# Second down product of a transformer kernel: last quarter of its depth by seven block products, final norm and output in column pieces

## The chip, the cores and the metric

The kernel runs on one core of one Trainium2 chip. The metric is the device time in microseconds (us) of one execution; the text writes ns where a number is in nanoseconds. Engines are named as in the profile: PE is TensorE's matmuls, PEld its weight loads, DVE is VectorE, ACT ScalarE, POOL GpSimd, SP SyncE, whose queue here only issues DMAs.

## What is computed

Two transformer blocks on 1024 tokens of width 1024, in fp32. The part that the change touches is the end of the second block and a small piece in its middle:

```python
def sqrelu_mlp(h, ln_g, w1, w2):
    u = rmsnorm(h, ln_g) @ w1            # 1024 -> 4096
    return jnp.square(jax.nn.relu(u)) @ w2   # 4096 -> 1024
...
        h = h + sqrelu_mlp(h, ln_ff_g[l], w_ff1[l], w_ff2[l])
    return rmsnorm(h, ln_final_g)
```

with `rmsnorm(x, g) = x * rsqrt(mean(x*x) + 1e-6) * g` over the 1024 features of a token. The small piece is the same norm over 128 values for each of four heads inside `bidirectional_gla`.

## The kernel before, in words

**Layout.** Activations lie with the feature on the partitions: `XB` holds the residual stream as eight row tiles of 128 features, each 1024 tokens wide. Every fp32 product is made of three passes: each operand is split into a high part (a rounding copy on ACT) and a low part (a subtraction on DVE), and PE adds high*high, high*low and low*high. A 128x128 weight block against 512 tokens is thus three matmuls.

**Two ways to make a product.** A *plain unit* (`pe_unit`, `product`, line 256) makes one row tile of the output, all 1024 tokens, from eight weight blocks: 8 x 3 x 2 = 48 matmuls of 512 columns. The *seven* way (`Seven` for the up products, `Down` for the down products) treats two row tiles by two column halves as a 2x2 block matrix and makes the four quarters of the result with seven block products instead of eight (the table `FACTORS`: weight factors A11, S1, S2, S4, S3, A12, A22 against data factors B11, T1, T2, B22, T3, B21, T4). S1 to S4 are sums of weight quarters made on DVE (`dve_dws`, lines 2639 to 2652, for the down product). T1 to T4 are sums of data quarters.

**Down product.** Its depth of 4096 is cut into groups of 1024. For each group `g` there are seven factors `i` and for each factor four products `p` (row pairs of the output), so 28 products of 12 matmuls of 512 columns (`pe_down_seven`, line 3143, its matmuls at 3158). Before, three groups go this way (`DOWN2_GROUPS = FF2_GROUPS - 1`, 84 products), and the last quarter of the depth is made by eight plain units (`pe_ff2_down`, line 3171); the last two of these, at line 3187, run in the column pieces 0:512, 512:768 and 768:1024 (`END_COLS`).

**Hidden layer and its sums.** The up product (`Seven` S2, `pe_seven`, matmuls at 3136) makes the 32 hidden tiles as 16 pairs `q`, seven products each. ACT squares the two tiles of a pair (`act_up_square`, 2559), SP stores them to the HBM array `hidden` (2859). For pairs 0 to 11 DVE also makes T1 to T4 with four operations of 512 columns in its slots 1, 2 and 3 of the next pair (`dve_t_sums`, 2539), into the tiles `TSUM`, and SP stores them in two DMAs of 512 KB to `hidden_t` (2875).

**Order of the work.** Nothing schedules at run time. Each engine runs a list written out by hand: a *slot* is one product of PE, and for it ACT makes a high weight part three products ahead (`act_dpw_hi`), DVE the low part (`dve_dpw_lo`, 2636), then ACT and DVE split one quarter `k` of the next data block (`act_block_hi`, `dve_block_lo`, 2620), then DVE makes a weight sum (`dve_dws`) and adds a finished product to `XB` (`dve_quad`, 2661). The engines are held together by semaphores, and a wait stops everything behind it on its engine.

**From the up to the down product.** In the last pair of the up product (`q = 15`, "slot 15,i" for its product i) the first data block B11 of the down product is loaded by SP (`sp_block`, 2910) as soon as product 15,0 is done, then four weight tiles of 1 MB (`sp_w4`, 2894) after 15,1 and 15,2, then blocks 1 and 2. ACT splits block 0 from slot 3 on (`HI_FIRST`); DVE makes the low parts of the first weights and of block 0 at the end of its slots 4, 5 and 6 (`dve_dpw_lo`, `dve_block_lo`). At the head of the same DVE slots stand the sums of the up product: `dve_sum12` (2411) in slot 4, `dve_sum22` (2417) in slot 5, for which PE's product 15,6 waits, `dve_sum11` (2421, 2428) in slot 6, `dve_sum21` (2438, 2439) after it. ACT's square of the last tile and its next high weight part follow `dve_sum21`.

**The end.** Each finished row tile is squared (ACT), the squares are added (DVE), PE multiplies the sum by a constant matrix, which leaves the mean over all features on every partition (3198, 3199), ACT takes the root as Ln (2774) and Exp (2776, scale -0.5), and DVE multiplies `XB` by weight and root into `Y` (3110), one operation for each row tile and piece. SP stores each at once (3248). In the head norm of `act_gla` the root is Ln (2029) and Exp (2032) as well.

## Time and profile before

| | |
|---|---|
| median of 3 runs | 2974.15 us (2974.0 to 2974.2) |
| profiled execution: its own time, its span | 2975.5 us, 2973.7 us |
| PE busy | 2909.8 us, 98% of the span |
| PEld, DVE, ACT, POOL busy | 81%, 67%, 48%, 16% |
| chain that ended last, by engine | PE 89%, DVE 4%, ACT 4%, issue 2% |
| DMA | 262.14 MB, mean 88 GB/s |

The page of the profile gives busy times by engine; a PE that is busy 98% of the span is not thereby at its peak, since its matmuls overlap. The chain follows the work back from the last instruction. The timeline and the stretches give start times from the start of the span.

### The profile page before, as it was taken

Reading aid. Unit: us, or ns where it says so; the run is one execution under the profiler, and the core shown is the slowest. Engines: PE = TensorE matmul, PEld = TensorE weight load, DVE = VectorE, ACT = ScalarE, POOL = GpSimd, SP = SyncE. Lnnn points to the kernel's source line nnn. Section 1 sums busy time; section 2 is a strip of 40 time slices with the busy share of each in tenths; the row PEclk is TensorE's granted clock in tenths of the full one; section 3 lists DMA queues with packets and bytes.
Section 4 is the critical chain, followed back from the end, with each engine's and each line's share of the span. In section 5 each row is a group of like instructions: output and inputs, shape, how many; then the busy total and the mean of one; then the engine's idle time right before and its main releaser. Section 6 shows DMA issues by size and latency. Waiting matters only on the chain.

```text
span 2973.7 us, 42637 instructions
## 1 busy us (share of the span) xinstructions
PE 2909.8 (98%) x16332; PEld 2413.5 (81%) x16332; DVE 1984.1 (67%) x3262; ACT 1441.8 (48%) x2411; POOL 467.7 (16%) x764
## 2 busy tenths in 40 slices
PE   9999999889999999999999999999999999999998
PEld 6888888778988887888878888777877788888887
DVE  6653246766775349999989852475654877778864
ACT  4552125887776126555444431375643544444432
POOL 0110004765554120000000010261012000000000
PEclk9999997999999999999999999999999999999999
DMA  4222231000000511333344332000101244464232
GB/s 150 73 84 71 85 114 43 2 1 2 2 2 7 207 43 64 114 114 114 114 160 157 116 111 92 28 2 36 43 30 72 104 165 168 157 241 156 99 114 71
DMA packets 85383, 262.14 MB, mean 88 GB/s; under 512 B 10448, under 2 KB 13648, under 8 KB 84800
## 3 DMA queue, kind: packets, MB, share of 16 engines
q1 hardware_dynamic: 74208, 219.29, 20.3%
q0 software_dynamic: 10976, 40.15, 3.8%
q8 instruction: 131, 2.15, 0.3%
q14 instruction: 68, 0.56, 0.1%
HBM read 187.58 MB, written 66.06 MB: 85 GB/s over the span
## 4 chain that ended last, share of the span: by engine, by line
PE 89%; DVE 4%; ACT 4%; issue 2%; POOL 0%; DMA 0%; SPq 0%; ACTq 0%; DVEq 0%; POOLq 0%
PE PS L256 33%; PE PS L3136 23%; PE PS L3158 12%; PE PS L919 3%; PE PS L933 3%; PE PS L905 2%; PE PS L904 2%; PE PS L280 1%; PE PS L1563 1%; PE PS L1598 1%; PE PS L1585 1%; ACT P_SHORT L1003 1%; PE PS L956 1%; PE PS L3187 1%; ACT PT L1013 1%
## 5 line engine op out<-in xcount | busy, mean ns | idle before, releaser
L223 ACT CAST WHI<-RAW 128x1024 fp32r<-128x1024 f32 x100 | 104.8, 1049 | 589.4 <-PE PS L256 569.6
L228 DVE TENSOR_TENSOR WLO<-RAW,WHI 128x1024 fp32r<-128x1024 f32 x102 | 125.5, 1231 | 361.4 <-ACT WHI L223 360.1
L256 PE MATMUL PS<-HLO,WHI 128*128 128x512 f32 x992 | 306.2, 390 | 0.0
L3136 PE MATMUL PS<-XSH_T,PWH 128*128 128x512 f32 x596 | 233.1, 391 | 5.4 <-DVE PWL L2396 2.4
L3136 PE MATMUL PS<-XSH_T,PWL 128*128 128x512 f32 x596 | 231.9, 389 | 0.0
L3136 PE MATMUL PS<-XSL_T,PWH 128*128 128x512 f32 x596 | 231.9, 389 | 0.0
L3158 PE MATMUL PS<-DXH,PWH 128*128 128x512 f32 x560 | 218.1, 389 | 1.4 <-DVE DXL L2620 1.3
L256 PEld LDWEIGHTS PS<-HLO,WHI 128*128 128x128 f32 x992 | 186.5, 188 | 39.2
L3158 PE MATMUL PS<-DXL,PWH 128*128 128x512 f32 x560 | 217.9, 389 | 0.0
L3158 PE MATMUL PS<-DXH,PWL 128*128 128x512 f32 x560 | 217.9, 389 | 0.0
L3136 PE MATMUL PS<-XSH_B,PWL 128*128 128x512 f32 x456 | 177.4, 389 | 0.0
L3136 PE MATMUL PS<-XSH_B,PWH 128*128 128x512 f32 x456 | 177.4, 389 | 0.0
L3136 PE MATMUL PS<-XSL_B,PWH 128*128 128x512 f32 x456 | 177.4, 389 | 0.0
L256 PE MATMUL PS<-HHI,WHI 128*128 128x512 f32 x512 | 160.5, 395 | 2.7 <-DVE WLO L228 2.7
L256 PE MATMUL PS<-HHI,WLO 128*128 128x512 f32 x512 | 158.4, 391 | 0.0
L2392 ACT CAST PWH<-WS_S 128x512 fp32r<-128x512 f32 x148 | 91.4, 617 | 129.1 <-PE PS L3136 115.8
L904 PE MATMUL PS<-KHD,QS 128*128 128x512 f32 (+3 forms) x384 | 138.8, 368 | 3.7 <-DVE KF L388 2.2
L3136 PEld LDWEIGHTS PS<-XSH_T,PWH 128*128 128x128 f32 x596 | 111.9, 188 | 30.8 <-DVE PWL L2396 4.2
L1114 POOL TENSOR_SCALAR P_LONG<-P_LONG,HINV,GATE 128x640 f32<-128x640 f32 (+3 forms) x128 | 121.5, 960 | 93.6 <-DVE HINV L1097 92.8
L1003 ACT ACTIVATE P_LONG<-P_LONG,HMIN 128x640 f32<-128x640 f32 (+3 forms) x128 | 116.8, 914 | 38.1 <-DVE HMIN L1092 37.4
L3136 PEld LDWEIGHTS PS<-XSH_T,PWL 128*128 128x128 f32 x596 | 111.9, 188 | 23.5
L3136 PEld LDWEIGHTS PS<-XSL_T,PWH 128*128 128x128 f32 x596 | 111.9, 188 | 23.4 <-issue 0.5
(443 smaller groups left out, 7225.6 us busy)
## 6 DMA issues: line engine op xcount, KB each, us to landing
W<-in_w SPq DMA_DIRECT2D x57, 1024.0 KB, 6.4
RAW<-in_w SPq DMA_DIRECT2D x104, 512.0 KB, 3.3
hidden<-W SPq DMA_DIRECT2D x54, 512.0 KB, 2.8
DXR<-hidden_t SPq DMA_DIRECT2D x20, 1024.0 KB, 5.1
DXR<-hidden SPq DMA_DIRECT2D x15, 1024.0 KB, 5.1
hidden_t<-W SPq DMA_DIRECT2D x24, 512.0 KB, 3.3
...
```

What stands on the lines that cost most here:

```text
L223: nc.scalar.copy(WHI[:, slot, :], RAW[:, slot, :]).then_inc(w_hi, 1)
L228: nc.vector.tensor_tensor(WLO[:, slot, :], RAW[:, slot, :], WHI[:, slot, :].bitcast(F32), ALU.subtract).then_inc(w_lo, 1)
L256: last = nc.tensor.matmul(o[:, half], w[:, slot, cols], x(k)[:, half], start=(k == 0 and w is WHI and x is hi), stop=(done and k == kcs - ...
L904: nc.tensor.matmul(out, QS[s % 2][:, j, :], KHD[g][:, branch, c:end], start=True, stop=False)
L905: last = nc.tensor.matmul(out, QS[s % 2][:, j, :], KLD[g][:, branch, c:end], start=False, stop=True)
L919: last = nc.tensor.transpose(turn_ps(c)[:, P * (2 * x + e):P * (2 * x + e) + P], src, IDENT[:, :])
L933: last = nc.tensor.matmul(out_ps(m)[half_of(e), :], (VS, VW)[branch][:, kt, g], PT[u % 8][:, 2 * x + e, :], start=False, stop=(u + 1 == us ...
L1003: nc.scalar.activation(p, p, ACT.Exp, scale=-1.0, bias=HMIN[:, n % 8, branch:branch + 1], accum_out=HSUM[:, n % 8, branch:branch + 1]).the ...
L1114: nc.gpsimd.tensor_scalar(p, p, HINV[:, n % 8, branch:branch + 1], GATE[:, qt, col:col + 1], ALU.mult, ALU.mult).then_inc(p_done, 1)
L2392: nc.scalar.copy(c.pwh[n % 4][:, :], c.raw_of(n)).then_inc(pw_hi, 1)
L3136: last = nc.tensor.matmul(c.banks[q % 2][b], wt[n % 4][:, cols], xt[x][:, k, :], start=(opens and k == 0 and xt is c.xsh and wt is c.pwh), ...
L3158: last = nc.tensor.matmul(DOWN_BANK(i, p), wt[:, cols], xt[:, k, :], start=(opens and k == 0 and wt is d.pwh(n) and xt is d.xh[r]), stop=( ...
```

## The change

The last quarter of the down product becomes a fourth group of the seven way: `DOWN2_GROUPS = FF2_GROUPS`. The eight plain units, their eight weight splits and eight data splits go. T sums are made and stored for all 16 pairs, those of pairs 12 to 14 in the up product, those of pair 15 in slots 1 to 3 of the down product. In SP's list the sums of pair 14 stand ahead of the first block load. The seventh factor of the last group (A22, T4) runs in two column pieces of 256; its eight pieces of 12 matmuls are followed by reads of PE's result in the order of `dve_end`. The residual columns 512:1024, finished one factor earlier, are squared in the slots of factors 4 and 5. The squares are added by POOL. The pieces of norm and output are columns 512:1024, 0:256, 256:512. Roots, here and in the head norm, are Sqrt on ACT and a reciprocal on DVE. Of the output rows of the first piece the last two are made by ACT and POOL.

```diff
@@ -2026,10 +2026,8 @@
-            nc.scalar.activation(ORS[:, h, :], OSUM[:, h, :], ACT.Ln, scale=1.0 / GLA_DV, bias=EPS_T[:, 0:1])\
+            nc.scalar.activation(ORS[:, h, :], OSUM[:, h, :], ACT.Sqrt, scale=1.0 / GLA_DV, bias=EPS_T[:, 0:1])\
                 .then_inc(gl_root, 1)
-            act.wait_ge(gl_root, 2 * h + 1)
-            nc.scalar.activation(ORS[:, h, :], ORS[:, h, :], ACT.Exp, scale=-0.5).then_inc(gl_root, 1)
...
     def dve_gla_norm(dve, h):
-        dve.wait_ge(gl_root, 2 * h + 2)
+        dve.wait_ge(gl_root, h + 1)
+        seq(dve, nc.vector.reciprocal(ORS[:, h, :], ORS[:, h, :]))
...
-    DOWN1_GROUPS, DOWN2_GROUPS = FF1_GROUPS - 1, FF2_GROUPS - 1
+    DOWN1_GROUPS, DOWN2_GROUPS = FF1_GROUPS - 1, FF2_GROUPS
...
@@ act_ff2_down @@
             if g == DOWN2_GROUPS - 1:
...
+                for m in END_SQUARES_AT.get((i, p), ()):
+                    act_end_square(act, m)
+                if (i, p) == (5, 2):
+                    for k in range(KC - N_POOL_ROWS, KC):
+                        act_prescale(act, k)
+                if (i, p) == (6, 0):
+                    break
+        for n in (11, 12, 13):
+            act_end_square(act, n)
+        act_end_root(act, 0)
+        for n in (14, 15, 16, 17):
+            act_end_square(act, n)
+        act_end_root(act, 1)
+        for n in (18, 19):
+            act_end_square(act, n)
+        act_end_root(act, 2)
@@ sp_seven2, for q in range(Q_LAST2) @@
             for b in range(2):
                 store(q, b)
-            if q < T2_PAIRS:
-                sp.wait_ge(t_sums, T_SUMS0 + 4 * q + 4)
-                for b in range(2):
-                    sp.dma_start(hidden_t[q, b], TSUM[b][:, :]).then_inc(D2.t_out, 16)
+            sp.wait_ge(t_sums, T_SUMS0 + 4 * q + 4)
+            for b in range(2):
+                sp.dma_start(hidden_t[q, b], TSUM[b][:, :]).then_inc(D2.t_out, 16)
         sp.wait_ge(pw_lo, S2.done(Q_LAST2 - 1, 6))
         sp.wait_ge(sums_done, S2.sums)
         sp.wait_ge(prod_done, S2.done(Q_LAST2, 0))
@@ sp_block @@
-            sp.wait_ge(d.t_out, d.t_out0 + 32 * 4 * d.groups)
+            sp.wait_ge(d.t_out, d.t_out0 + 32 * pairs.stop)
@@ sp_ff2_down, after the weights of group 1 @@
+        sp.wait_ge(t_sums, T_SUMS0 + 4 * FF2_PAIRS)
+        for b in range(2):
+            sp.dma_start(hidden_t[Q_LAST2, b], TSUM[b][:, :]).then_inc(D2.t_out, 16)
...
+    HI_END, END_A, END_B = HI_COLS, slice(0, 256), slice(256, 512)
+    END_PIECES = (HI_END, END_A, END_B)
...
+    def act_end_root(act, i):
+        cols = END_PIECES[i]
+        n = cols.stop - cols.start
+        act.wait_ge(end_mean, END_MEAN0 + i + 1)
+        nc.scalar.activation(ROOT[:, cols], bank(END_BANK[i])[:, 0:n], ACT.Sqrt, bias=EPS_T[:, 0:1]).then_inc(end_root, 1)
+
+    def pool_end(pool):
+        for r, n in enumerate(END_SUMMED):
+            cols, k = END_SQUARES[n]
+            if r == END_SUMMED_IN[1]:
+                pool.wait_ge(end_rstd, END_RSTD0 + 1)
+                for j in range(N_POOL_ROWS):
+                    y = Y[:, KC - N_POOL_ROWS + j, HI_END]
+                    pool.wait_ge(prescaled, PRESCALED0 + j + 1)
+                    nc.gpsimd.tensor_tensor(y, y, END_RSTD_HI, ALU.mult).then_inc(scaled_by_pool, 1)
+            pool.wait_ge(end_sq, END_SQ0 + n + 1)
+            if r:
+                pool.wait_ge(end_sum, END_SUM0 + r)
+            nc.gpsimd.tensor_tensor(END_SUM[:, cols], END_SUM[:, cols], SQ_RING[r % 4][:, 0:cols.stop - cols.start],
+                                    ALU.add).then_inc(end_sum, 1)
+
+    def dve_end_z(dve, p):
+
+        row = XB[:, 2 * p + 1, END_B]
+        dve.wait_ge(prod_done, D2.prod0 + 28 * (DOWN2_GROUPS - 1) + 16 + p + 1)
+        nc.vector.tensor_tensor(row, row, bank(4 + p)[:, END_B], ALU.add).then_inc(end_z, 1)
+
+    def dve_end_quad(dve, b, p):
+
+        cols, at_bank = ((END_A, 4), (END_B, 0))[b]
+        row = XB[:, 2 * p + 1, cols]
+        dve.wait_ge(end_prod, END_PROD0 + 4 * b + p + 1)
+        if b:
+            dve.wait_ge(end_z, END_Z0 + p + 1)
+        nc.vector.tensor_tensor(row, row, bank(at_bank + p)[:, END_A], ALU.add).then_inc(end_quad, 1)
+
+    def dve_end_rstd(dve, i):
+        cols = END_PIECES[i]
+        dve.wait_ge(end_root, END_ROOT0 + i + 1)
+        nc.vector.reciprocal(RSTD_END[i], ROOT[:, cols]).then_inc(end_rstd, 1)
+        dve.wait_ge(end_rstd, END_RSTD0 + i + 1)
+        if i:
+            dve.wait_ge(end_quad, END_QUAD0 + 4 * i)
+        else:
+            dve.wait_ge(D2.quads, quad_at(4, 3))
+
+    def dve_end_scale(dve, i, rows):
+        for k in rows:
+            nc.vector.scalar_tensor_tensor(Y[:, k, END_PIECES[i]], XB[:, k, END_PIECES[i]], NORM_W[:, 4, k:k + 1],
+                                           RSTD_END[i], ALU.mult, ALU.mult).then_inc(y_done, 1)
+
+    def dve_end(dve):
+        for p in range(3):
+            dve_end_quad(dve, 0, p)
+        dve_end_rstd(dve, 0)
+        dve_end_scale(dve, 0, range(0, 2))
+        dve_end_quad(dve, 0, 3)
+        dve_end_scale(dve, 0, range(2, 4))
+        dve_end_quad(dve, 1, 0)
+        dve_end_scale(dve, 0, range(4, 5))
+        dve_end_quad(dve, 1, 1)
+        dve_end_scale(dve, 0, range(5, 6))
+        dve_end_quad(dve, 1, 2)
+        dve_end_rstd(dve, 1)
+        dve_end_scale(dve, 1, range(0, 2))
+        dve_end_quad(dve, 1, 3)
+        dve_end_scale(dve, 1, range(2, KC))
+        dve_end_rstd(dve, 2)
+        dve_end_scale(dve, 2, range(KC))
+
+    def pe_end_mean(pe, i):
+        cols = END_PIECES[i]
+        out = bank(END_BANK[i])[:, 0:cols.stop - cols.start]
+        pe.wait_ge(end_sum, END_SUM0 + END_SUMMED_IN[i])
+        pe.wait_ge(end_sq, END_SQ0 + (8, 16, 20)[i])
+        pe.wait_ge(end_quad, END_QUAD0 + i + 1)
+        last = nc.tensor.matmul(out, ONES[:, :], END_SUM[:, cols], start=True, stop=(i == 0))
+        if i:
+            last = nc.tensor.matmul(out, ONES[:, :], SQ_LAST[:, cols], start=False, stop=True)
+        last.then_inc(end_mean, 1)
+
+    def pe_end_product(pe, b, p):
...
+        cols, at_bank = ((END_A, 4), (END_B, 0))[b]
...
+            for wt, xt in ((D2.pwh(n), D2.xh[r]), (D2.pwh(n), D2.xl[r]), (D2.pwl(n), D2.xh[r])):
+                last = nc.tensor.matmul(bank(at_bank + p)[:, END_A], wt[:, w], xt[:, k, cols],
...
+    def pe_end(pe):
+        for b in range(2):
+            for p in range(4):
+                pe_end_product(pe, b, p)
+                if p == 1:
+                    pe_end_mean(pe, b)
+        pe_end_mean(pe, 2)
@@ dve_seven2 @@
             dve_seven_slot(dve, S2, j)
-            if 1 <= q <= T2_PAIRS:
+            if q:
                 dve_t_sums(dve, q - 1, i)
@@ dve_ff2_down, at the end of a slot @@
+            if g == 0 and i == 0 and p:
+                dve_t_sums(dve, Q_LAST2, p)
+            if (g, i) == (DOWN2_GROUPS - 1, 5):
+                dve_end_z(dve, p)
+            if (g, i, p) == (DOWN2_GROUPS - 1, 6, 0):
+                break
+        dve_end(dve)
...
```

## Rows read from the trace of the kernel before

**Rows 1.** Stretches by stage: us, busy us (count) by engine, PEclk, DMA share, GB/s
```profile
2627.30:2643.70 16.40, 16.40 (x74) 13.56 (x73) 8.98 (x13) 7.91 (x14) 0.00 (x0) 1.00 1.00 385
...
2656.40:2872.30 215.90, 215.89 (x952) 178.75 (x953) 186.27 (x284) 93.34 (x159) 0.00 (x0) 1.00 0.39 142
2872.30:2937.60 65.30, 65.30 (x290) 54.07 (x289) 22.67 (x20) 14.49 (x14) 0.00 (x0) 1.00 0.12 45
2937.60:2962.90 25.30, 25.17 (x152) 21.86 (x151) 12.36 (x18) 11.63 (x15) 0.00 (x0) 1.00 0.18 66
```

**Rows 2.** Chain that ended last, from 2840 us: start, us, what
```profile
2872.31 65.28 PE PS L256 x288
2937.59 12.31 PE PS L3187 x60
...
2950.01 1.10 PE PS L3198 x2
...
2951.96 5.75 PE PS L3187 x48
...
2962.92 0.43 DVE XB L3099
...
2963.81 1.28 ACT L2774
...
2965.59 1.28 ACT L2776
...
2967.34 0.48 DVE Y L3110
```

**Rows 3.** Timeline of SP, its DMA issues: start, us, line, out<-in, count
```profile
2578.51 0.93 SPq L2875 DMA_DIRECT2D hidden_t<-W  x2
...
2627.33 0.37 SPq L2910 DMA_DIRECT2D DXR<-hidden  x1
2629.84 3.60 SPq L2894 DMA_DIRECT2D W<-in_w  x4
```

**Rows 4.** Timeline of ACT around the third weight tile of the down product
```profile
2641.74 0.62 ACT L2632 CAST PWH<-W 128x512 fp32r<-128x512 f32 x1 [2.26 <-DMA W<-in_w]
```

**Rows 5.** Timeline of DVE in slots 15,5 and 15,6
```profile
2638.01 0.69 DVE L2417 TENSOR_TENSOR W<-PART,PS 128x512 f32<-128x512 f32 x1 [0.27 <-PE PS L3136]
...
2642.59 0.68 DVE L2636 TENSOR_TENSOR PWL<-W,PWH 128x512 fp32r<-128x512 f32 x1
```

**Rows 6.** Chain that ended last, from 2627 us: the first factor of the down product
```profile
2647.31 0.69 DVE PWL L2636
...
2648.61 0.61 DVE S L2644
...
2656.41 3.74 PE PS L3158 x15
```

**Rows 7.** Groups of DVE instructions by line: all reciprocals but those of 2 elements
```profile
L1688 DVE RECIPROCAL NINV<-NSUM 128x1 f32<-128x1 f32 x64 | 9.8, 154 | 0.4 <-ACT PN L1628 0.4
...
L1174 DVE RECIPROCAL CINV<-CSUM 128x8 f32<-128x8 f32 x15 | 3.0, 203 | 0.5
```

**Rows 8.** Timeline of DVE at the end, the output rows of two pieces
```profile
2956.98 5.38 DVE L3110 SCALAR_TENSOR_TENSOR Y<-XB,NORM_W,W 128x512 f32<-128x512 f32 x8
...
2963.59 3.25 DVE L3110 SCALAR_TENSOR_TENSOR Y<-XB,NORM_W,W 128x256 f32<-128x256 f32 x8
```

**Rows 9.** Groups of POOL instructions by line and form: one addition of 512 columns
```profile
L2292 POOL TENSOR_TENSOR XSR_T<-XB 128x512 f32<-128x512 f32 x4 | 5.5, 1379 | 0.1
```

**Rows 10.** Waits of DVE around the head norm: us in total, times, longest us
```profile
DVE ON L2056 <- ACT ORS L2032: 3.8, 2, 1.9
```

**Rows 11.** Stretches of 4 us around short stops of PE (columns as rows 1)
```profile
36.00:40.00 4.00, 1.32 (x6) 0.94 (x6) 3.27 (x4) 2.43 (x5) 0.00 (x0) 0.97 0.04 12
40.00:44.00 4.00, 4.00 (x13) 3.15 (x12) 3.93 (x7) 0.00 (x0) 0.00 (x0) 0.60 0.38 139
44.00:48.00 4.00, 4.00 (x16) 2.64 (x15) 2.54 (x4) 0.07 (x1) 0.00 (x0) 1.00 0.30 115
```

More of the change, by code:

```diff
@@ L2280, in build @@
               [x_in_used(3), x_in_used(4)], hid2_hi, hid2_lo, hid_hi, 28 * DOWN1_GROUPS + FF1_REST, x_in[2],
-              x_in_used(2), [R + 32 * KB + 8 * KB * k for k in range(4)] +
-              [X_AT + 16 * KB, X_AT + 24 * KB, R, R + 8 * KB], FF2_TILES - KC, KC)
+              x_in_used(2), [], 0, 0)
     TSUM = [W[0], W[2]]
@@ L2910, in sp_block, with sp_ff2_down @@
         sp.dma_start(d.xr[b % 4][:, :, :], src).then_inc(d.block_in[b % 4], 16)
-    def sp_plain2(sp, k):
-        sp.wait_ge(hid_out[k % 2], 16 * ((FF1_TILES, 0)[k % 2] + FF2_PAIRS))
-        if k >= 4:
-            sp.wait_ge(prod_done, D2.prods - (12, 12, 8, 8)[k - 4])
-            sp.wait_ge(D2.lo, 4 * D2.blocks + k - 3)
-        else:
-            sp.wait_ge(D2.lo, 4 * (D2.blocks - 4 + k) + 4)
-        sp.dma_start(D2.plain_raw[k][:, :], hidden[FF2_TILES - KC + k]).then_inc(D2.block_in[(D2.blocks + k) % 4], 16)
-    def sp_ff2_down(sp, load):
+    def sp_ff2_down(sp):
         sp.wait_ge(up_done, S2.ups)
@@ L2933, in sp_ff2_down @@
                 for p in range(4):
-                    sp_w4(sp, D2, 2, p)
-        for k in range(2):
-            sp_plain2(sp, k)
-        sp.wait_ge(pw_lo, D2.prods - 8)
-        for t in range(2):
-            u = U_FF2 + t
-            sp.dma_start(RAW[:, u % 2, :], a["w"][stored_down(FF2_TILES - KC + t)]).then_inc(w_loaded[u % 2], 16)
-        for k in range(2, KC):
-            sp_plain2(sp, k)
-        for t in range(2, KC):
-            load(U_FF2 + t, stored_down(FF2_TILES - KC + t))
@@ new lines, in build @@
+    END_SUMMED = [n for n, (cols, k) in enumerate(END_SQUARES) if n != 0 and n != KC and not (n >= 12 and k == 7)]
+    END_SUMMED_IN = (7, 13, 16)
+    SQ_RING = [W[0][:, LO_COLS], W[0][:, HI_COLS], W[3][:, LO_COLS], W[3][:, HI_COLS]]
+    SQ_LAST, END_SUM, ROOT = W[4][:, HI_COLS], W[2], W[1]
+    END_RSTD_HI = W[4][:, LO_COLS]
+    END_RSTD_LO = sb("END_RSTD_LO", [512], R + 96 * KB)
+    RSTD_END = [END_RSTD_HI, END_RSTD_LO[:, END_A], END_RSTD_LO[:, END_B]]
+    end_sq, end_sum, end_mean, end_root, end_rstd = sq_done, acc_done, mean_done, ln_done, rstd_done
@@ new lines, in act_end_square @@
+    def act_end_square(act, n):
+        cols, k = END_SQUARES[n]
+        act.wait_ge(*final_at(n))
+        if n in END_SUMMED:
+            r = END_SUMMED.index(n)
+            if r >= 4:
+                act.wait_ge(end_sum, END_SUM0 + r - 3)
+            dst = SQ_RING[r % 4][:, 0:cols.stop - cols.start]
+        elif n >= 12:
+            dst = SQ_LAST[:, cols]
+        else:
+            dst = END_SUM[:, cols]
+        nc.scalar.activation(dst, XB[:, k, cols], ACT.Square).then_inc(end_sq, 1)
@@ new lines, in pe_end_product @@
+    def pe_end_product(pe, b, p):
+        n, r = D2.n - 4 + p, (D2.blocks - 1) % 4
+        cols, at_bank = ((END_A, 4), (END_B, 0))[b]
+        pe.wait_ge(pw_lo, D2.prod0 + n + 1)
+        if b:
+            pe.wait_ge(D2.quads, quad_at(5, p))
+        else:
+            pe.wait_ge(end_z, END_Z0 + p + 1)
+            pe.wait_ge(D2.quads, quad_at(4, p))
+        for k in range(4):
+            if b == p == 0:
+                pe.wait_ge(D2.lo, 4 * (D2.blocks - 1) + k + 1)
+            w = slice(k * P, k * P + P)
+            for wt, xt in ((D2.pwh(n), D2.xh[r]), (D2.pwh(n), D2.xl[r]), (D2.pwl(n), D2.xh[r])):
+                last = nc.tensor.matmul(bank(at_bank + p)[:, END_A], wt[:, w], xt[:, k, cols],
+                                        start=(b == 1 and k == 0 and wt is D2.pwh(n) and xt is D2.xh[r]),
+                                        stop=(k == 3 and wt is D2.pwl(n)), skip_group_check=True)
+        last.then_inc(end_prod, 1)
@@ L3141, in pe_seven, with pe_down_seven @@
                 pe_mean(pe, c.norm)
-    def pe_down_seven(pe, d, z_free):
-        for n, (g, i, p) in enumerate(d.products):
+    def pe_down_seven(pe, d, z_free, end):
+        for n, (g, i, p) in enumerate(d.products[:end]):
             opens = i in (0, 1, 5)
@@ L3243, in _ @@
         sp_seven2(sp)
-        sp_ff2_down(sp, load)
-        for i, (a0, a1) in enumerate(END_COLS):
+        sp_ff2_down(sp)
+        for i, cols in enumerate(END_PIECES):
             for k in range(KC):
-                sp.wait_ge(y_done, KC * i + k + 1)
-                sp.dma_start(out[k][:, a0:a1], Y[:, k, a0:a1]).then_inc(out_done, 16)
-        sp.wait_ge(out_done, 16 * KC * len(END_COLS))
+                if i == 0 and k >= KC - N_POOL_ROWS:
+                    sp.wait_ge(scaled_by_pool, POOL_SCALED0 + k - (KC - N_POOL_ROWS) + 1)
+                else:
+                    sp.wait_ge(y_done, KC * i - (N_POOL_ROWS if i else 0) + k + 1)
+                sp.dma_start(out[k][:, cols], Y[:, k, cols]).then_inc(out_done, 16)
+        sp.wait_ge(out_done, 16 * KC * len(END_PIECES))
     @block.gpsimd
```

137 lines of the change are left out of this document (36 added, 101 removed).

## Prediction

> **What bounds the kernel now.** I read the stretches by stage first. PE is busy 215.89 of 215.9 us in the down product's seven way and 65.30 of 65.3 us in the first six plain units [rows 1]; DVE has 186.27 us of work in the former, so it follows PE with little to spare. 288 matmuls of 512 columns take 65.28 us, 0.2267 us each, and 48 of 256 columns take 5.75 us, 0.12 us each [rows 2]. (The mean of one that a group of the page shows is longer, because matmuls overlap.) Then the chain from 2840 us: PE without a gap to 2962.9, then one read of its result, a square, a table load, Ln, a table load, Exp, eight output rows, and the span ends at 2973.7, 6.36 us after the first of these rows starts [rows 2]. Last the queue of SP where the up product meets the down product, since the change moves loads there: block 0 of the data is issued at 2627.33, the weights from 2629.84 [rows 3], the DMA engines are full at 385 GB/s [rows 1], and ACT stands waiting for the third weight tile until 2641.74 [rows 4]. This place is already tight: PE restarts at 2656.41 just when DVE delivers [rows 6].
>
> The profiled span is 2973.7 us, its execution 2975.5; the median is 2974.15. I work out a difference in span and add it to the median. A difference of 0.2%, 5.95 us, is about what a measurement can tell from none.
>
> **1. Matmuls.** Before, the last quarter has 6 x 48 + 48 matmuls of 512 columns and 96 of 256 [rows 1, 2]. After, it has 24 products x 12 = 288 of 512 and 8 pieces x 12 = 96 of 256. 48 of 512 columns go: 48 x 0.2267 = 10.9 us of PE, all on the path.
>
> **2. Extra splits, weight sums, blocks, T sums in the up product.** A fourth group costs DVE what a group costs now: 186.27 us over some 79 products is 2.35 us in a slot of 2.72 us [rows 1]. It stays hidden; without that cover each slot would cost up to the difference. The T sums of pairs 12 to 14 are four operations of 0.6 us in slots where DVE has 7.4 of 16.4 us free [rows 1]. Zero.
>
> **3. SP's queue at the last pair.** SP now waits for the T sums of pair 14 and issues two stores before block 0 of the down product. The sums of pair 11 are issued at 2578.51 [rows 3]; a pair takes 84 x 0.2267 = 19.04 us, so those of pair 14 go at 2635.6. With 0.93 us for two issues [rows 3], block 0 goes at 2636.5 in place of 2627.33: 9.2 us late. Behind it stand four weight tiles and block 1, all in a full bus. Another 0.5 MB of stores is ahead of it (at 385 GB/s 1.35 us, less the 0.45 us that it starts earlier): 0.9 us. The third weight tile lands at 2641.74 + 10.1 = 2651.8.
>
> Who waits: DVE makes the low part of weight 0 and of block 0 at the end of slot 4, ahead of `dve_sum22` of slot 5. That sum ran at 2638.01 [rows 5]; now it follows the first weight tile, which the same 10 us bring to some 2646, with a split on ACT and two operations on DVE behind it: about 2648. PE's product 15,6 waits for it, so PE stands from 2640.9 to 2648, 7 us. Next late: the low part of weight 2, at 2642.59 [rows 5] only 0.2 us after its data could allow, then the rest of block 0, `dve_sum21`, ACT's square, weight 3. The row of weight 3 at 2647.31 [rows 6] moves by 10.1 - 0.2 = 9.9 us.
>
> **4. T sums of pair 15** stand in DVE's slots 1 to 3 of the down product, where DVE is the chain: three of the four operations come before the last quarter of block 1, at a pitch of 0.61 us [rows 6]: 1.8 us. PE, which resumed at 2656.41, resumes at 2668.1. The fourth eats the 0.14 us a slot that DVE then gains (slots of 2.58 against 2.72 us). Parts 3 and 4 together: **11.7 us** lost. Bounds: 0, if the loads are hidden after all; 14, if nothing overlaps with the extra stores and the fourth sum counts too. I take 11.7, since rows 3 to 6 give each term. The stores of pair 15 stand after the weights of group 1 and before block 4, which is needed eleven products later: zero, as long as the bus empties by then.
>
> **5. The end**, from E, the end of product (5,3) of the last group. PE needs 8 x 1.44 us and a mean of up to 1.10 us [rows 2] after pieces 2 and 6. ACT's first root waits for the square after piece 2 (3.8), loads a table of 1.28 us, and takes 0.7 us: 5.8. POOL's additions, 1.379 us for 512 columns [rows 9], seven of them over four slots, are done before; its two scaled rows, 2.8 us, too, before SP comes to them.
> No row shows a reciprocal over many columns. One element takes 154 ns, eight take 203 [rows 7], 7.0 ns for each more. That gives 3.7 us for 512 columns and 1.9 for 256. The other bound is the pace of an addition, 0.7 and 0.4 us. I take the slope, because it comes from the same instruction.
> DVE then: first reciprocal to 9.5; six output rows at 5.38 / 8 = 0.67 us and five reads at 0.42 to 15.1; second reciprocal to 17.1; two rows at 0.41 [rows 8] and a read to 18.3; six rows to 20.7; the last root is ready at 20.2; third reciprocal to 22.7; then the 6.36 us of the last eight rows and stores [rows 2]. The end is at E + 29.1. (PE stops about 2 us before its second mean; piece 7 is still done before DVE asks.) DVE is the bound here, not PE.
> Before, the same point is 2937.59 and the end 2973.7: 36.1 us. With part 1 in it, the end thus gains 7.0 us. The two table loads of 1.28 us in the last chain [rows 2] are in that: one reciprocal of 1.9 us and no load stand against Exp of 0.42 us and two loads.
> The Trainium skill (ScalarE: Activation LUTs, section on table sets) says that Ln and then Exp need one load, since one set has both. The chain shows one ahead of each [rows 2], so the row decides. By the page the change would save no load in the last chain, and the last root would be 2.6 us dearer against before; my sum would be +7.3.
>
> **6. Head norm.** DVE waited 1.9 us twice for the root [rows 10]; a root is about 2.5 us shorter on ACT, but PE is behind other work in all but the last head, and a reciprocal of 0.2 us with its wait is added where DVE leads. Bounds -0.6 and +0.8; zero.
>
> **Sum:** +11.7 - 7.0 = +4.7 us in span; 2974.15 + 4.7, rounded, is **2979.0 us**.
>
> **Rivals.**
> A, *the loads are hidden anyway*: parts 3 and 4 cost less than 1.0 us. For it: the weights are needed one for each 2.72 us only. Against: ACT waits for them now. Then the gain of 7.0 us stands: 2967.2, faster. It decides below 1.0 us in place of 11.7.
> B, *cheap reciprocal*: at the pace of an addition three of them save 3.0 + 1.5 + 1.5 = 6.0 us, DVE's chain ends at E + 23: 2973, no change. Against it is the slope.
> C, *half clock*: after a stretch with PE busy 1.32 of 4 us, a dense stretch ran at 0.60, between its levels of 1.2 and 2.4 GHz, and the next at 1.00 [rows 11]. PE stands 7 us in part 3 and twice 2 to 3 us in the end. In part 3 half speed is mostly behind DVE's chain (up to +1.4); at the end, second mean, piece 7 and the last mean at half speed reach DVE's list 1.8 and 0.5 us late: +3.7 in all, 2982.6, slower. It decides from 1.2 us on. The Trainium skill (TensorE: Matmul & The Clock Gate, part 1) has it that the idle clock is the slow one and work releases it; by that rule C is certain in part 3 and likely at the end.
> D, *the change doesn't do what it says*: DVE's lag after part 4 does not shrink and takes PE with it all through the group, or the fourth group is bound by DVE: some +3 more; I count it with C.
>
> **Chances.** My forecast 0.45 (of which a third, with a part of C, lies above +5.95); A, or most of A, 0.10; B 0.15; C and D 0.20; parts 3 and 4 at about half 0.10. Faster 0.10, same 0.55, slower 0.35. The range leaves out the outer half of A and of C with D: 2968 to 2985.5. The forecast's own range is 2976.5 to 2981.5.
>
> **What would show it.** Right: block 0 issued near 2636.5 behind two stores; `dve_sum22` near 2648; PE idle some 7 us before product 15,6 and again about 2 us in the fourth product of the down product; its seven way 11 to 12 us later than before; reciprocals of 3.7 and 1.9 us; DVE without a gap from the first root to the end; one table load in the end. Wrong: PE full at 2641 to 2648, or reciprocals under 1 us. It would also be wrong if ACT loaded tables more than once there.

## The result, and the profile after

Before 2975.26 us (median of 14 runs, 2972.59 to 2978.34), after 2982.62 us (14 runs, 2978.53 to 2984.69). The ratio is 1.0025, its 95% interval 1.0018 to 1.0032: slower by 7.4 us. The profiled span grew from 2973.7 to 2982.2 us, by 8.5. (The kernel before measured 1.1 us more here than in the three runs ahead of the prediction.)

Stages before the changed one shift by up to 3 us between executions, so below I measure ways between two points of one trace: from the start of SP's store of the hidden tiles of pair 14 (2624.76 before, 2624.84 after), and from E, the end of product (5,3) of the last group (in the kernel before, the end of the sixth plain unit, 2937.59). The way from E to the end also differs between executions of the same code: four kernels whose end is the same, those of after and of experiments 2, 3 and 4, have 33.9, 32.4, 33.7 and 33.1 us.

The page of after, its first section, the groups of the down product's matmuls and of the up product's, with the costliest wait at the end of the row:

```profile
PE 2902.3 (97%) x16282; PEld 2406.3 (81%) x16282; DVE 2035.3 (68%) x3354; ACT 1441.7 (48%) x2442; POOL 490.0 (16%) x782
...
L3255 PE MATMUL PS<-DXH,PWH 128*128 128x512 f32 x656 | 255.6, 390 | 1.7 <-DVE DXL L2617 1.7
...
L3233 PE MATMUL PS<-XSH_T,PWH 128*128 128x512 f32 x596 | 234.2, 393 | 12.9 <-DVE W L2414 7.6
```

PE is busy 7.5 us less than before (2909.8), and the span is 8.5 us longer. One wait of 7.6 us stands out. SP's queue where the up product meets the down product (start, us, line, out<-in, count), the answer to [rows 3]:

```profile
2635.12 1.27 SPq L2869 DMA_DIRECT2D hidden_t<-W  x2
2636.58 0.37 SPq L2904 DMA_DIRECT2D DXR<-hidden  x1
2636.99 2.88 SPq L2888 DMA_DIRECT2D W<-in_w  x4
```

Block 0 goes out at 2636.58 behind the two stores, in place of 2627.33. DVE, in the same stretch (in brackets the idle time before and what ended it), the answer to [rows 5]:

```profile
2646.34 0.69 DVE L2633 TENSOR_TENSOR PWL<-W,PWH 128x512 fp32r<-128x512 f32 x1 [10.27 <-ACT PWH L2629]
2646.95 0.68 DVE L2617 TENSOR_TENSOR DXL<-DXR,DXH 128x512 fp32r<-128x512 f32 x1
2647.55 0.68 DVE L2414 TENSOR_TENSOR W<-PART,PS 128x512 f32<-128x512 f32 x1
...
2656.79 0.69 DVE L2633 TENSOR_TENSOR PWL<-W,PWH 128x512 fp32r<-128x512 f32 x1 [1.63 <-ACT PWH L2629]
...
2661.19 0.68 DVE L2545 TENSOR_TENSOR W<-W 128x512 f32<-128x512 f32 x1
2661.79 0.69 DVE L2546 TENSOR_TENSOR W<-W,W 128x512 f32<-128x512 f32 x1
```

DVE stands 10.27 us for the first weight tile, then makes two low parts and only then the sum (L2414) for which PE's product 15,6 waits. The T sums of pair 15 (L2545, L2546) stand between the parts that PE waits for. The chain picks PE up at 2667.34, against 2656.41 [rows 6], and from there PE has no gap to the end of the last full factor (chain: start, us, what; its row ends at 2934.89, PE's own rows go on without a gap to E):

```profile
2667.34 267.55 PE PS L3255 x1179
```

E is 2948.31, against 2937.59 before: +10.7 us. From E to the end of the span it is 33.9 us, against 36.1: -2.2. The sum is +8.5.

DVE from the first reciprocal on, the answer to [rows 8]:

```profile
2955.28 3.35 DVE L3016 RECIPROCAL W<-W 128x512 f32<-128x512 f32 x1
2958.66 3.53 DVE L3025 SCALAR_TENSOR_TENSOR Y<-XB,NORM_W,W 128x512 f32<-128x512 f32 x2
...
2962.45 1.40 DVE L3025 SCALAR_TENSOR_TENSOR Y<-XB,NORM_W,W 128x512 f32<-128x512 f32 x2
...
2967.72 0.42 DVE L3011 TENSOR_TENSOR XB<-XB,PS 128x256 f32<-128x256 f32 x1 [1.74 <-PE PS L3073]
2968.05 1.74 DVE L3016 RECIPROCAL END_RSTD_LO<-W 128x256 f32<-128x256 f32 x1
...
2974.18 1.75 DVE L3016 RECIPROCAL END_RSTD_LO<-W 128x256 f32<-128x256 f32 x1 [0.76 <-ACT W L2977]
2975.97 3.26 DVE L3025 SCALAR_TENSOR_TENSOR Y<-XB,NORM_W,END_RSTD_LO 128x256 f32<-128x256 f32 x8
```

The reciprocals take what was forecast (3.35 and 1.75 us for 3.7 and 1.9). But the first two output rows take 3.53 us where two others of the same form take 1.40, and DVE stands 1.74 us for a product of PE and 0.76 us for the last root. POOL at the time of the slow rows:

```profile
2958.70 2.94 POOL L2991 TENSOR_TENSOR Y<-Y,W 128x512 f32<-128x512 f32 x2 [2.08 <-DVE W L3016]
```

and the clock there (stretches of 4 us: busy us and count of PE, PEld, DVE, ACT, POOL, then PEclk, DMA share, GB/s):

```profile
2954.00:2958.00 4.00, 4.00 (x36) 4.00 (x35) 3.06 (x2) 1.62 (x3) 1.50 (x3) 1.00 0.00 0
2958.00:2962.00 4.00, 1.22 (x11) 1.01 (x9) 3.96 (x3) 0.00 (x0) 2.94 (x2) 0.91 0.15 57
2962.00:2966.00 4.00, 2.93 (x10) 2.60 (x11) 3.98 (x8) 1.61 (x4) 1.03 (x2) 0.50 0.63 233
```

and PE's second mean (two of its four matmuls; in brackets the idle time before):

```profile
2963.07 1.19 PE L3053 MATMUL PS<-W,ONES 128*128 128x256 f32 x2 [3.85 <-issue]
```

PE stood 3.85 us before it, since DVE read the pieces late: the mean waits for the square of piece 4, which DVE reads at 2962.11, after the two slow rows. PE came back at 0.50, its level of 1.2 GHz.

### The profile page after: what moved, and what is told of

It is laid out like the page before. It is cut to its first block, busy times and chain, and to the rows that moved or that the text cites. A ratio compares the mean times of both kernels' runs of the same rounds, so it can differ in the third digit from the quotient of the medians.

```text
span 2982.2 us, 42761 instructions
## 1 busy us (share of the span) xinstructions
PE 2902.3 (97%) x16282; PEld 2406.3 (81%) x16282; DVE 2035.3 (68%) x3354; ACT 1441.7 (48%) x2442; POOL 490.0 (16%) x782
## 4 chain that ended last, share of the span: by engine, by line
PE 87%; DVE 5%; ACT 4%; issue 2%; DMA 1%; POOL 1%; SPq 0%; POOLq 0%; DVEq 0%; ACTq 0%
PE PS L256 30%; PE PS L3233 23%; PE PS L3255 14%; PE PS L919 3%; PE PS L933 3%; PE PS L904 2%; PE PS L905 2%; PE PS L1563 1%; PE PS L1598 1%; PE PS L1585 1%; PE PS L956 1%; ACT P_SHORT L1003 1%; PE PS L280 1%; ACT PT L1013 1%; PE PS L947 1%
## 5 line engine op out<-in xcount | busy, mean ns | idle before, releaser
L228 DVE TENSOR_TENSOR WLO<-RAW,WHI 128x1024 fp32r<-128x1024 f32 x94 | 115.7, 1231 | 361.0 <-ACT WHI L223 360.2
L223 ACT CAST WHI<-RAW 128x1024 fp32r<-128x1024 f32 x94 | 98.4, 1048 | 539.5 <-PE PS L256 519.9
L3255 PE MATMUL PS<-DXH,PWH 128*128 128x512 f32 x656 | 255.6, 390 | 1.7 <-DVE DXL L2617 1.7
L3255 PE MATMUL PS<-DXL,PWH 128*128 128x512 f32 x656 | 255.2, 389 | 0.0
L3255 PE MATMUL PS<-DXH,PWL 128*128 128x512 f32 x656 | 255.2, 389 | 0.0
L3255 PEld LDWEIGHTS PS<-DXH,PWH 128*128 128x128 f32 x656 | 123.3, 188 | 27.9 <-DVE DXL L2617 2.6
L3255 PEld LDWEIGHTS PS<-DXL,PWH 128*128 128x128 f32 x656 | 123.3, 188 | 25.7
L3255 PEld LDWEIGHTS PS<-DXH,PWL 128*128 128x128 f32 x656 | 123.1, 188 | 25.8
```

Source lines behind the costliest of these rows:

```text
L223: nc.scalar.copy(WHI[:, slot, :], RAW[:, slot, :]).then_inc(w_hi, 1)
L228: nc.vector.tensor_tensor(WLO[:, slot, :], RAW[:, slot, :], WHI[:, slot, :].bitcast(F32), ALU.subtract).then_inc(w_lo, 1)
L3255: last = nc.tensor.matmul(DOWN_BANK(i, p), wt[:, cols], xt[:, k, :], start=(opens and k == 0 and wt is d.pwh(n) and xt is d.xh[r]), stop=( ...
```

## The experiments

The theory after these readings: the stores ahead of block 0 cost some 9 us, pair 15's sums 1.8; at the end POOL's multiplications hold DVE up, and the stop of PE that follows costs its clock. Rivals: the loads were not the cause but DVE's order; the end is short of its forecast for the reciprocals alone. Where no baseline is named, an edit is made to the kernel after; its ratio is to the kernel before.

**1. The queue alone.** In the kernel before, T sums of pairs 12 to 14 too:

```diff
-    T1_PAIRS, T2_PAIRS = DOWN1_GROUPS * GROUP // 2, DOWN2_GROUPS * GROUP // 2
+    T1_PAIRS, T2_PAIRS = DOWN1_GROUPS * GROUP // 2, FF2_PAIRS - 1
```

> The kernel before, with the sums T1 to T4 made and stored for pairs 0 to 14 in place of 0 to 11, and nothing else; the stores of pair 14 then stand ahead of block 0 in SP's list. Queue theory: block 0 is issued at about 2636.6 us in place of 2627.3, PE stands 7 to 8 us before product 15,6, and the first factor of the down product restarts at about 2665.5 in place of 2656.4; span +9 us. Rival (the sums of pair 15 on DVE, which this kernel doesn't have, are what costs): PE without a stop, span within 2 us of before.

2984.44 us, ratio 1.003 (1.0017 to 1.0042). Block 0 is issued at 2636.08. The waits of PE from 2620 to 2680 us (total, times, longest), and the chain behind them:

```profile
PE PS L3136 <- DVE W L2417: 7.8, 1, 7.8
```
```profile
2647.67 4.81 PE PS L3136 x12
2652.48 228.53 PE PS L3158 x1008
```

Three pairs' sums, of which this kernel uses nothing, cost nearly what the whole transition costs: PE's first matmul of the down product starts 28.3 us after the store of pair 14, against 18.5 before. Of these 9.9 us, 7.8 is the wait, and some 2 that product 15,6 then takes 4.81 us in place of 12 x 0.2267 = 2.72. To E it is 322.3 us from that store, against 312.8 before and 323.5 in the kernel after: 9.5 of the 10.6 us.

**2. Loads ahead of the stores.** SP issues the stores of pair 14 behind block 1:

```diff
-            sp.wait_ge(t_sums, T_SUMS0 + 4 * q + 4)
-            for b in range(2):
-                sp.dma_start(hidden_t[q, b], TSUM[b][:, :]).then_inc(D2.t_out, 16)
+            if q < Q_LAST2 - 1:
+                store_sums(q)
...
         sp_block(sp, D2, 1)
+        store_sums(Q_LAST2 - 1)
```

> The kernel after, with SP's two stores of pair 14 moved behind the loads of blocks 0 and 1 and of the four weight tiles. Queue theory: block 0 at 2627.3 again, no stop of PE before product 15,6; what is left of the loss is the three DVE operations of pair 15, so that PE restarts in the first factor at about 2658.2 (before: 2656.4, after: 2667.3); span 9 us under that of after. Rival (the bus is full with the additional stores wherever they stand): the third weight tile still lands after 2648, span at most 4 us under after.

2975.8 us, ratio 1.000 (0.999 to 1.001). Block 0 is issued at 2628.06, there is no stop at 15,6, and the restart comes 34.4 us after the store of pair 14, against 42.5 in the kernel after and 31.65 before. So at the restart 8.1 us of the 10.85 were the queue's order. But PE now stands 2.05 us right before the restart, where it stood 0.4 in the kernel after (waits of PE, and the chain):

```profile
PE PS L3260 <- DVE DXL L2617: 2.4, 2, 2.0
```
```profile
2659.88 269.20 PE PS L3260 x1179
```

After this stop the clock is at 0.68 from 2660 to 2664 us, and the 1179 matmuls take 269.20 us where they took 267.55 in the kernel after. So to E it is 317.0 us from the store of pair 14, against 323.5: 6.5 us returned, not 8.1, nor the 9 that I expected (medians 2982.6 and 2975.8, a difference of 6.8).

**3. And the sums of pair 15 later**, in factor 4 of the first group, their stores behind block 7:

```diff
-            if g == 0 and i == 0 and p:
+            if g == 0 and i == 4 and p:
                 dve_t_sums(dve, Q_LAST2, p)
```

> As after_loads_first, and DVE's sums of pair 15 moved from the slots of the first factor to those of the fifth, where it makes no weight sums; their stores behind block 7. If each sum at the head costs its 0.6 us on the path, PE restarts at 2656.4 as before and the span is 1.8 us under that of after_loads_first. Rival (DVE has room there or loses it elsewhere): the same span within 0.5 us.

2972.18 us, ratio 0.9986 (0.9977 to 0.9996). The restart comes at 32.6 us, 1.8 earlier than in the run before it: the three sums of 0.6 us. PE's stop is 1.0 us in place of 2.05 and the clock stays at 1.00, so another 1.65 us come back: to E it is 313.6 us, 3.4 less than in the run before it, and the median is 3.6 less, where I expected 1.8. What is left, 0.95 us against before at the restart and 0.75 at E, hangs on block 1: the chain of this run goes through its transfer, beside full DMA engines.

**4. DVE's order alone.** The low parts of the first weight and block behind the sum that 15,6 waits for:

```diff
-                if i >= 4:
+                if i == 5:
+                    dve_dpw_lo(dve, D2, 0)
+                    dve_block_lo(dve, D2, 0, 0)
+                if i >= 5:
...
```

> The kernel after, with VectorE's low parts of the first block and first weight moved behind the sum of pair 14 that the second product's factor 15, 6 waits for (about 2647 in the kernel after). Theory: the low parts have to be made before the down product's first factor in any case and the transfers they need arrive no earlier, so TensorE's stop only moves: none or under 2 us ahead of factor 15, 6, and 5 us or more ahead of the down product; the restart in its first factor stays at 42 to 43 us from the start of the store of pair 14, and the span stays at 2979 to 2984. Rival: the order on VectorE was the cost and not the transfers: the restart comes 4 us or more earlier (38 or less from the same point), and the span is 5 us shorter than that of the kernel after.

2983.57 us, ratio 1.002 (1.0008 to 1.0033), span 2984.6. PE's waits there, and the chain:

```profile
PE PS L3258 <- DVE DXL L2617: 6.5, 3, 4.0
```
```profile
2641.77 9.80 DMA W<-in_w
2651.57 0.02 issue
2651.59 0.63 ACT PWH L2629
```

The stop before 15,6 is gone, and 6.5 us of stops stand in the down product instead, the longest 4.0. My expectation of a restart at 42 to 43 us was wrong in its form: the chain leaves DVE already at 2656.65, 28.2 us after the store of pair 14, because PE then runs at the low clock (0.67, 0.50 and 0.55 in the three stretches from 2650 to 2662 us) and has become the slower of the two. By the letter of my expectation this was the rival's restart; but the span is not 5 us shorter, and E is 323.1 us from that store, against 323.5 in the kernel after: the order moves the loss and returns 0.4 us of it. The transfers are the cause.

**5. The two multiplications of POOL left out.** The output rows 6 and 7 of columns 512 to 1023 are not multiplied by the root:

```diff
-                    nc.gpsimd.tensor_tensor(y, y, END_RSTD_HI, ALU.mult).then_inc(scaled_by_pool, 1)
...
-                    sp.wait_ge(scaled_by_pool, POOL_SCALED0 + k - (KC - N_POOL_ROWS) + 1)
+                    sp.wait_ge(prescaled, PRESCALED0 + k - (KC - N_POOL_ROWS) + 1)
```

> The kernel after without POOL's two multiplications (the output rows 6 and 7 of columns 512 to 1023 are left without the root). Theory, that POOL's instructions hold up DVE's: the two output rows that took 3.53 us together beside POOL's multiplications take 1.4 us, and the way from the start of the first reciprocal to the end, 26.9 us in the kernel after, is 2 to 3 us shorter. Rival (DVE's rows are slow for their operands or for the stores beside them): they take 3.5 us again and the way stays within 0.5 us. The low part of the data blocks beside POOL's additions, 1.78 us in place of 0.68, stays in either case, since the additions stay.

2978.16 us, ratio 1.0012 (1.0003 to 1.0022). DVE, the rows that took 3.53 us:

```profile
2951.83 3.35 DVE L3012 RECIPROCAL W<-W 128x512 f32<-128x512 f32 x1
2955.21 1.41 DVE L3021 SCALAR_TENSOR_TENSOR Y<-XB,NORM_W,W 128x512 f32<-128x512 f32 x2
```

From the start of the first reciprocal to the end it is 22.3 us in place of 26.9: 2.1 from the rows, 2.5 because PE's stop is shorter (1.73 us in place of 3.85), its clock stays at 1.00 until 2965, and DVE no longer stands for piece 7.

**6. PE kept busy.** 26 and 18 products of 256 columns, whose result nobody reads, ahead of the second and the third mean:

```diff
+                    if b:
+                        pe_idle_work(pe, 1, 26)
                     pe_end_mean(pe, b)
+        pe_idle_work(pe, 2, 18)
         pe_end_mean(pe, 2)
```

> The kernel after, with 26 matmuls of 256 columns ahead of the second mean and 18 ahead of the third, whose results the mean overwrites: PE works where it stood idle. Clock theory: the granted clock stays at 1.00 from 2958 to 2972, the last mean takes 0.9 us in place of 2.06, the read of piece 7 no longer waits 1.7 us for PE, and the end is 2.5 to 3 us earlier. Rival (DVE and POOL set the end): span within 0.7 us of after.

2981.91 us, ratio 1.0018 (1.0008 to 1.0027). Stretches, and the last mean (its second line is L3055, 0.59 us):

```profile
2962.00:2966.00 4.00, 3.37 (x29) 3.16 (x27) 4.00 (x4) 0.36 (x1) 2.73 (x2) 1.00 0.18 66
2966.00:2970.00 4.00, 3.84 (x29) 3.77 (x30) 4.00 (x8) 1.67 (x5) 1.69 (x3) 1.00 0.72 266
```
```profile
2972.87 0.67 PE L3053 MATMUL PS<-W,ONES 128*128 128x256 f32 x2 [0.58 <-issue]
```

With POOL's work as it was, the way from the first reciprocal to the end is 24.3 us, 2.6 shorter than the 26.9 of after: the waits of 1.74 and 0.76 us, for piece 7 and for the last root, are gone. That is what the low clock cost in that one execution. In the traces of experiments 2, 3 and 4, whose end is that of after, the same way is 25.4, 26.7 and 26.1 us, so the price is 1.1 to 2.6 us: in experiment 2 the second mean ran at full speed after the same stop of 3.85 us (0.67 us, where the other three have 1.19). The ratio's interval overlaps that of after, so the medians neither confirm nor deny it, and the statement rests on the traces.

**7. Roots by logarithm at the end**, ACT's Ln and Exp in place of Sqrt and DVE's reciprocal:

```diff
-        nc.scalar.activation(ROOT[:, cols], bank(END_BANK[i])[:, 0:n], ACT.Sqrt, bias=EPS_T[:, 0:1]).then_inc(end_root, 1)
+        nc.scalar.activation(ROOT[:, cols], bank(END_BANK[i])[:, 0:n], ACT.Ln, bias=EPS_T[:, 0:1]).then_inc(end_root, 1)
+        act.wait_ge(end_root, END_ROOT0 + i + 1)
+        nc.scalar.activation(RSTD_END[i], ROOT[:, cols], ACT.Exp, scale=-0.5).then_inc(end_rstd, 1)
```

> The kernel after with the three last roots by Ln and Exp on ACT, as in the kernel before, in place of Sqrt and a reciprocal; all else as it is. The reciprocals of 3.35, 1.75 and 1.75 us are on the path, two table loads of 1.28 us and an Exp of 0.4 to 0.6 us take their place on ACT. Theory: the first output row starts 1.5 us earlier after the first mean, the last one some 2 us earlier, the end 2 to 3 us earlier. Rival (the loads cost as much as the reciprocals, which was the reason for them in the sum): the way from the first mean to the end within 0.7 us of after.

2981.72 us, ratio 1.0024 (1.0014 to 1.0033). ACT's first root:

```profile
2952.51 1.28 ACT L2977 ACT_TABLE_LOAD   x1
2953.80 0.69 ACT L2977 ACTIVATE W<-PS,EPS_T 128x512 f32<-128x512 f32 x1
2954.51 1.28 ACT L2979 ACT_TABLE_LOAD   x1
2955.80 0.63 ACT L2979 ACTIVATE W<-W 128x512 f32<-128x512 f32 x1
```

DVE, the first output rows of each piece:

```profile
2956.47 1.90 DVE L3025 SCALAR_TENSOR_TENSOR Y<-XB,NORM_W,W 128x512 f32<-128x512 f32 x2 [1.82 <-ACT W L2979]
...
2967.05 1.35 DVE L3025 SCALAR_TENSOR_TENSOR Y<-XB,NORM_W,END_RSTD_LO 128x256 f32<-128x256 f32 x2 [2.85 <-ACT END_RSTD_LO L2979]
...
2973.60 3.26 DVE L3025 SCALAR_TENSOR_TENSOR Y<-XB,NORM_W,END_RSTD_LO 128x256 f32<-128x256 f32 x8 [2.49 <-ACT END_RSTD_LO L2979]
```

The loads are not hidden: DVE stands 7.2 us for the three roots, where the three reciprocals took it 6.84. From the read of piece 3 to the end it is 25.6 us in place of 27.3; but the traces of experiments 2, 3 and 4, whose end is that of after, have 25.8, 27.0 and 26.4. So a gain of 1.7 us by the logarithm is not shown, nor are the 2 to 3 us that I expected, and the medians agree (2981.72 and 2982.62, the ratios 1.0024 and 1.0025): the two kinds of root cost about the same here.

**8. Head norm alone**, Sqrt and reciprocal there in the kernel before:

```diff
-            nc.scalar.activation(ORS[:, h, :], ORS[:, h, :], ACT.Exp, scale=-0.5).then_inc(gl_root, 1)
...
+        seq(dve, nc.vector.reciprocal(ORS[:, h, :], ORS[:, h, :]))
```

> The kernel before with the roots of the head norm by Sqrt and a small reciprocal, as the change has them. Theory (PE is behind other work there): the stretch from the last matmul ahead of the head norm to the first of the full output units is within 0.5 us of before. Rival (the roots are on the path): 2 us shorter or more.

One execution, so its time says little: 2976.61 us. The stretch from the plain products at 2182.15 us in the trace of before to those at 2252.39 takes 70.24 us; here 70.32, in the kernel after 70.49. Nothing, or 0.1 to 0.25 us lost.

**9. POOL's additions cut to one column each.** The output's norm then lacks most of its squares; number and order of instructions stay.

```diff
-            nc.gpsimd.tensor_tensor(END_SUM[:, cols], END_SUM[:, cols], SQ_RING[r % 4][:, 0:cols.stop - cols.start],
+            at = slice(cols.start, cols.start + 1)
+            nc.gpsimd.tensor_tensor(END_SUM[:, at], END_SUM[:, at], SQ_RING[r % 4][:, 0:1],
```

> The kernel after, with GpSimd's additions of squares in the output's norm cut to one column each, so the output's norm lacks most of its squares; the number of instructions and their order stay. Theory: VectorE's subtraction for the low part of the last block takes longer when it runs beside a GpSimd instruction that reads on-chip memory: the two rows of it fall from 1.78 us to about 0.7 us, and TensorE's wait of 0.7 us for them at the end of the sweeps goes. The output rows that run beside GpSimd's two multiplications still take about 3.5 us for the two. The way from the last sweep to the end gets 0.5 to 1.5 us shorter, 32.4 to 33.4 us in place of 33.9. Rival: the subtraction is long for another reason (its operand or its place): it stays at 1.5 us or more.

2981.63 us, ratio 1.0023 (1.0013 to 1.0033), span 2976.9. DVE's subtraction for the last block and its sum with PE's result, first in the kernel after, where POOL's L2995 runs from 2948.12 for 3.23 us, then here:

```profile
2948.42 1.78 DVE L2617 TENSOR_TENSOR DXL<-DXR,DXH 128x512 fp32r<-128x512 f32 x1
...
2950.45 0.68 DVE L2658 TENSOR_TENSOR XB<-XB,PS 128x512 f32<-128x512 f32 x1
```
```profile
2944.25 0.69 DVE L2617 TENSOR_TENSOR DXL<-DXR,DXH 128x512 fp32r<-128x512 f32 x1
...
2945.65 0.69 DVE L2658 TENSOR_TENSOR XB<-XB,PS 128x512 f32<-128x512 f32 x1 [0.39 <-PE PS L3256]
...
2954.81 3.52 DVE L3026 SCALAR_TENSOR_TENSOR Y<-XB,NORM_W,W 128x512 f32<-128x512 f32 x2
```

The subtraction falls from 1.78 to 0.69 us, PE's wait of 0.7 us for it is gone, and the output rows beside the multiplications, which stayed, still take 3.52. DVE starts its first reciprocal 5.97 us after E, where the four kernels with the end of after have 6.96 or 6.97: this 1.0 us is what the additions cost ahead of the first root. From E to the end it is 31.5 us, less than the 32.4 to 33.4 expected: the last mean also ran at full clock (0.67 and 0.59 us), which it doesn't do in every execution. The median (2981.63) shows no such gain.

**10. All of it put right**: edits 2, 3 and 7, no output rows on POOL, and the reads of PE's pieces spread between the output rows:

```diff
-    N_POOL_ROWS = 2
+    N_POOL_ROWS = 0
...
-        for p in range(3):
+        for p in range(4):
             dve_end_quad(dve, 0, p)
         dve_end_rstd(dve, 0)
-        dve_end_scale(dve, 0, range(0, 2))
-        dve_end_quad(dve, 0, 3)
-        dve_end_scale(dve, 0, range(2, 4))
+        dve_end_scale(dve, 0, range(0, 1))
         dve_end_quad(dve, 1, 0)
-        dve_end_scale(dve, 0, range(4, 5))
+        dve_end_scale(dve, 0, range(1, 3))
```

> The change mended at all three places: SP's stores of pair 14 behind the first loads, the sums of pair 15 in the fifth factor, and an end with Ln and Exp, in which DVE reads pieces 1 to 4 ahead of the first output rows and scales all rows itself, without POOL's two. Theory: the transition costs 1 us in place of 10.9; the end takes some 25.5 us from product (5,3) of the last group (before 36.1, after 33.9), PE without a stop of over 1 us until its last piece and so at full clock; against before 2974 - 9 or so, 2965 to 2967. Rival (the parts don't add up, since the end is bound by SP's stores or by DVE): no lower than 2970.

2967.18 us (2964.12 to 2968.95), ratio 0.9972 (0.9961 to 0.9983): by the ratio 8.3 us less than before; the median is 15.4 under that of after. To E it is 313.6 us from the store of pair 14. E to the end is 27.9 us, not the 25.5 expected. How these 6 us under after divide between the rows taken from POOL, the order of the reads and the roots was not tried singly. Its chain shows where the transition still hangs, and what is last at the end:

```profile
2634.59 12.96 DMA DXR<-hidden_t
...
2954.26 0.77 POOLq L3475
2955.08 1.22 PE PS L3057 x2
2956.30 0.87 PE PS L3059 x2
```

Block 1 takes 12.96 us on a shared bus; and POOL's last addition is followed by a mean at the low clock, 2.09 us.

**11. The same with PE kept busy** by 20 products ahead of the last mean:

```diff
+        pe.wait_ge(end_quad, END_QUAD0 + 3)
+        for _ in range(20):
+            nc.tensor.matmul(bank(END_BANK[2])[:, END_A], D2.pwh(D2.n - 1)[:, 0:P], D2.xh[(D2.blocks - 1) % 4][:, 0, END_A],
```

> The version with the loads ahead of the stores, pair 15's sums late, the logarithm and exponential at the end and no output rows on GpSimd, plus 20 products of 256 columns on TensorE ahead of the last mean, whose result nobody reads. Theory: the last mean's two matmuls there took 2.09 us because TensorE had stood before them and its granted clock was down (0.50 in the 5 us around them); kept busy they take 0.9 to 1.1 us, the clock is over 0.9 in that stretch, and the way from the read of piece 3 to the end falls from 21.3 to about 20.2 us; the median is 1 us under the 2967.2 of the version without them, 2966, if the earlier stages do not cover it. Rival: the added products end after the squares' sum is ready, and push the last mean back by what they save: the way stays at 21 us or more.

2967.29 us (2966.49 to 2970.35), ratio 0.9971 (0.996 to 0.9982). Chain:

```profile
2954.81 0.70 PE PS L3057 x2
2955.51 0.45 PE PS L3059 x2
```

The mean takes 1.15 us in place of 2.09, the clock is 1.00 from 2940 to 2960 us, and from the read of piece 3 the last eight rows start 14.2 us later in place of 15.1. The end comes only 0.65 us earlier (20.65 against 21.3 us from that read), since 6.5 us in place of 6.2 pass from the rows' start to the end, and the median doesn't move. Not worth its lines.

## Why the prediction was right, and where it was off

The median came out at 2982.6, inside the range, and slower, to which I gave 0.35. My likeliest case was 2979.0, and the measured time lies 1.1 us above that case's own range of 2976.5 to 2981.5. Against the kernel before I forecast +4.7, and it is +7.4 by the medians and +8.5 by the two spans. Point by point:

**Matmuls (1) and hidden work (2).** Right. The down product runs without a gap from 2667.34 to E, so a fourth group is hidden by DVE's spare time, and rival D's lag of DVE did not appear.

**SP's queue (3) and pair 15 (4).** Right in mechanism and nearly in size: block 0 at 2636.58 (forecast 2636.5), the sum for 15,6 at 2647.55 (2648), PE's stop 7.6 us (7), restart 2667.34 (2668.1), 10.9 us lost in place of 11.7. Experiments 1 to 3 show the parts, at the restart: 8.1 for the order of the queue, 1.8 for pair 15's sums, 0.95 that stays with the added stores, in block 1's transfer, for which my sum had no term. At E the same three steps are 6.5, 3.4 and 0.75 us, since the clock fell between the first two. Experiment 4 shows that it is the transfers, not DVE's order. Two details were off. My 0.9 us for the bytes of the stores took 0.5 MB, and they are 1 MB; yet the third weight tile is ready 9.1 us later than before (2650.81 for 2641.74), no more than the 9.25 us by which block 0 is issued late. And the second stop of about 2 us, in the fourth product of the down product, was 0.4 us, which fits that PE had taken 5.26 us for product 15,6 in place of 2.72, at the low clock, and came to it late.

**The end (5).** This step failed in its size: forecast E + 29.1, measured E + 33.9, a gain of 2.2 us and not 7.0. What it lacked was the cost of POOL's work beside DVE's, and the low clock after the stop that came of it.
- I placed POOL's two scaled rows beside DVE's output rows at no cost. They cost 2.1 us of DVE (experiment 5), and the additions beside the split of the last block another 0.7 us of PE's start, 1.0 us at the first reciprocal (experiment 9).
- "Piece 7 is still done before DVE asks" was wrong. DVE, late by these, read PE's pieces late, PE stood 3.85 us, and the clock fell. That is rival C at the place I gave it. My main sum left it out; the rival had 1.8 and 0.5 us for the end, and DVE waited 1.74 and 0.76 in this trace (together 1.0 to 2.5 us in the four traces that have this end).
- The rows show a subtraction of two tiles in on-chip memory at 1.78 us beside POOL and 0.69 without, and a sum with PE's result at 0.68 both ways. The Trainium skill (GPSIMD Engine Reference, section Key points) says that GpSimd shares its memory interfaces with VectorE and gets in the way of VectorE instructions with two inputs there; the trace agrees.

The reciprocal, the one price that no row showed, was sized well by the slope of [rows 7]: 3.35 and 1.75 us for 3.7 and 1.9. Rival B is out. So is A: the loads were not hidden. A slip in the sum did no harm: five reads at 0.42 us would end at 15.6, not 15.1; `dve_end` has four there, and with four it is 15.2.

**Tables.** [rows 2] show a load ahead of each of Ln and Exp, and so did all six calls of experiment 7. The rule of the Trainium skill (ScalarE: Activation LUTs, section on table sets), by which the pair needs one, is not borne out by this kernel. The end of after has one load, as forecast. Experiment 7 shows that leaving out the logarithm gained nothing that can be measured: what DVE no longer waits for the two loads and the exponential, it spends on the reciprocal.

**Head norm (6).** Zero was forecast, 0.1 to 0.25 us found.

Together: +10.7 at E and -2.2 behind it give the 8.5 us of span, where I had +11.7 and -7.0. The 4.8 us by which the end was longer than forecast can be read off the trace of after: the first reciprocal starts 1.2 us late (E + 6.97 for 5.8; 1.0 of it goes with POOL's additions), two output rows take 2.1 more, DVE waits 1.7 for piece 7 and 0.8 for the last root, and three reciprocals (6.84 us in all) are 0.7 shorter than my 7.5; the small rest, 0.3, goes the same way. That rival C's 2982.6 is the measured time is partly luck: its share in part 3, up to 1.4 us, did not come, POOL's share of some 3 us was in no rival, and the transition was 1.0 us cheaper than my sum.

What stays open: how far block 1's last 0.95 us can be taken off the path, and what decides whether PE comes back from the same stop at full or at half speed. A different order of blocks and weights in the bus was not tried.
